# Expert weights of a mixture-of-experts kernel: rows regrouped to 4 KB pieces, and at most two pieces of 1 MB in flight

## What is computed

```python
h = rmsnorm(x, ln2_g[l]) * (1.0 + scale2) + shift2
probs = softmax(xt @ router_w);  sel = probs + router_b        # 64 experts, pick 1 group of 8, top 2 inside
def expert_block(args):
    xb, e = args
    return (jax.nn.silu(xb @ w1[e]) * (xb @ w3[e])) @ w2[e]    # w1, w3: 1024x512, w2: 512x1024
y = y.at[t_s].add(yp[dest] * w_s[:, None]);  x = x + gate2 * y;  return rmsnorm(x, final_g)
```

## Time and profile before

| | us |
|---|---|
| median of 3 runs (lowest, highest) | 1820.02 (1812.35, 1824.44) |
| the profiled execution, its own time | 1824.44 |
| its span, first to last instruction | 1822.6 |
| TensorE busy | 1229.9 (67%) |
| VectorE busy | 456.4 (25%) |
| chain that ended last: the stores `ys_dram<-arena` | 55% of the span |

### The profile page before, as it was taken

How to read it: one execution, slowest core, us unless ns; L and a number is a source line. 1 busy time by engine, 2 the same in 40 slices (tenths; PEclk the granted TensorE clock), 3 DMA queues, 4 the chain that set the end, 5 groups by cost and what they waited for, 6 DMA issues and landing times.

```text
span 1822.6 us, 31309 instructions
## 1 busy us (share of the span) xinstructions
PE 1229.9 (67%) x12648; PEld 649.3 (36%) x12649; DVE 456.4 (25%) x880; ACT 213.1 (12%) x537; POOL 182.9 (10%) x319
## 2 busy tenths in 40 slices
PE   4999999999455545767646585656645656754680
PEld 3544546455322322333323343323322323322340
DVE  1399763235511101111101120101110101100126
ACT  2300132111110000001000010000000000000014
POOL 2011200000010100101000011101001101100013
PEclk8999999999587776978877798777777878876795
DMA  9364704521988797777898649897889896699627
GB/s 353 143 208 139 280 0 162 182 93 61 366 340 338 305 422 306 304 295 266 346 421 329 265 181 418 327 415 294 341 343 416 322 421 255 235 420 413 261 95 279
DMA packets 104984, 517.72 MB, mean 284 GB/s; under 512 B 8745, under 2 KB 25657, under 8 KB 87416
## 3 DMA queue, kind: packets, MB, share of 16 engines
q1 hardware_dynamic: 78976, 471.04, 64.2%
q0 software_dynamic: 11984, 32.33, 5.0%
q10 hardware_dynamic: 13992, 13.90, 2.3%
HBM read 482.22 MB, written 35.01 MB: 284 GB/s over the span
## 4 chain that ended last, share of the span: by engine, by line
DMA 58%; PE 34%; DVE 5%; ACT 1%; issue 1%; ACTq 0%; SPq 0%; POOL 0%; POOLq 0%; DVEq 0%
DMA ys_dram<-arena 55%; PE banks L547 9%; PE banks L625 6%; PE banks L692 6%; PE banks L681 4%; PE banks L575 2%; DVE arena L1221 2%; PE banks L593 2%; DMA arena<-xh_dram,where 1%; PE banks L495 1%; DMA arena<-in_w_ada 1%; DMA arena<-in_x 1%; PE banks L641 1%; PE banks L698 1%; DVE arena L1251 0%
## 5 line engine op out<-in xcount | busy, mean ns | idle before, releaser
L692 PE MATMUL banks<-arena 128*32 128x256 f32 x3392 | 301.4, 516 | 450.2 <-DVE arena L1221 450.2
L681 PE MATMUL banks<-arena 128*32 128x256 f32 x6784 | 409.3, 395 | 27.4 <-issue 25.4
L692 PEld LDWEIGHTS banks<-arena 128*32 128x32 f32 x3392 | 138.3, 142 | 559.1 <-issue 528.3
L681 PEld LDWEIGHTS banks<-arena 128*32 128x32 f32 x6784 | 215.8, 114 | 189.6 <-issue 63.6
L1221 DVE TENSOR_TENSOR arena<-banks,arena 128x256 f32<-128x256 f32 x106 | 45.1, 426 | 841.3 <-DMA ys_dram<-arena 796.3
L547 PE MATMUL banks<-arena 128*128 128x512 f32 x352 | 157.4, 605 | 3.6 <-ACT arena L781 3.6
L443 POOL COPY where<-quarters 128x1 int32 (+1 forms) x108 | 19.9, 184 | 1222.7 <-ACT arena L855 1053.6
L841 ACT ACTIVATE arena<-banks 128x128 f32<-128x128 f32 x106 | 29.6, 279 | 849.7 <-issue 705.0
L969 DVE SCALAR_TENSOR_TENSOR arena<-arena 128x1024 f32<-128x1024 f32 x90 | 115.6, 1285 | 3.2
L446 POOL DMA_INDIRECT arena<-xh_dram,where x108 | 104.8, 970 | 87.7 <-POOL where L443 81.7
L625 PE MATMUL banks<-arena 128*128 128x512 f32 x256 | 111.4, 593 | 1.5 <-DVE arena L1002 1.5
(11 more groups left out here) (201 smaller groups left out, 667.5 us busy)
## 6 DMA issues: line engine op xcount, KB each, us to landing
arena<-in_exp_w SPq DMA_DIRECT2D x180, 2048.0 KB, 14.9
arena<-in_w_ada SPq DMA_DIRECT2D x12, 2048.0 KB, 11.2
arena<-in_exp_w SPq DMA_DIRECT2D x24, 1024.0 KB, 13.9
ys_dram<-arena ACTq DMA_DIRECT2D x106, 128.0 KB
ys_dram<-arena POOLq DMA_DIRECT2D x16, 512.0 KB, 10.0
arena<-in_x SPq DMA_DIRECT2D x2, 2048.0 KB, 19.9
arena<-in_dft SPq DMA_DIRECT2D x1, 4096.0 KB, 12.4
arena<-in_w_out SPq DMA_DIRECT2D x1, 4096.0 KB, 14.4
```

The costliest lines, as they stand in the source:

```text
L681: last = pe.matmul(h_p[32 * q:32 * q + 32, 0:2 * P].rearrange("p (a b) -> p a b", a=2), xt_s[:, k % 2, k // 2, :], w13[:, :, k, q * P:(q + ...
L692: last = pe.matmul(y_p[32 * q:32 * q + 32, 0:QUART], ff_t[:, k * BLK:(k + 1) * BLK], w2[:, k, q * QUART:(q + 1) * QUART], start=(k == 0), ...
```

## The change

- The channel order becomes 256q+2p+j everywhere. `w_in`, `router_w`, the columns of `ln_g`, `b_ada` and the modulation, `w1` and `w3` are loaded in that order; `chunk` takes every second channel of a quarter, `quarter_chunk` goes, and L1142 writes without a permutation. `w_in` and the router are now four transfers for each one before. The products for the first four slices of `w_ada` read contiguous columns where they read every fourth.
- `matrix` goes. All weights, in the loop too, are loaded in pieces of 1 MB: six for an expert, each 128 partitions x 2 runs of 4 KB. Each piece has a semaphore of its own.
- Before SP issues a piece in the loop it waits until the piece two before it (`AHEAD = 2`) has landed. The waits for the slot (`s_h13`, `s_yp`) stay.

```diff
+AHEAD = 2
         def d_cols(vector):
-            return vector.rearrange("(p k) -> p k", k=CH)
+            return vector.rearrange("(q p j) -> p q j", q=4, j=2)
...
         def chunk(view, k):
-            return view[:, k:D:CH]
-
-        def quarter_chunk(view, k):
             first = QUART * (k // 2) + k % 2
             return view[:, first:first - k % 2 + QUART:2]
...
-        s_w = [[sem(f"slot{i}_{what}_in") for what in ("w1", "w3", "w2")] for i in range(SLOTS)]
+        s_w = [[sem(f"slot{i}_{what}_in") for what in ("w1a", "w1b", "w3a", "w3b", "w2a", "w2b")] for i in range(SLOTS)]
...
-                sp.dma_start(w_in_s[:, :, f0:f1], w_in.rearrange("(p k) f -> p k f", k=CH)[:, :, f0:f1]).then_inc(s_win[part], 16)
+                for q in range(4):
+                    sp.dma_start(w_in_s[:, 2 * q:2 * q + 2, f0:f1],
+                                 w_in[q * QUART:(q + 1) * QUART, f0:f1].rearrange("(p j) f -> p j f", j=2)
+                                 ).then_inc(s_win[part], 16)
...
-                    src = (exp_w1, exp_w3)[u][bass.ds(e, 1), :, :].rearrange("e (p h c) f -> (e p) h (c f)", p=P, h=2)[:, h, :]
+                    src = (exp_w1, exp_w3)[u][bass.ds(e, 1), h * 512:(h + 1) * 512, :].rearrange("e (q p j) f -> (e p) q (j f)", q=2, j=2)
...
-                    sp.wait_ge(s_h13, end)
-                    for u in range(2):
-                        matrix(r * SLOTS + (SLOTS + slot), slot, u)
-                    sp.wait_ge(s_yp, end)
-                    matrix(r * SLOTS + (SLOTS + slot), slot, 2)
+                    for k in range(6):
+                        if k == 0:
+                            sp.wait_ge(s_h13, end)
+                        if k == 4:
+                            sp.wait_ge(s_yp, end)
+
+                        before, rounds = (slot, r + 2) if k >= AHEAD else ((slot - 1) % SLOTS, r + (2 if slot else 1))
+                        sp.wait_ge(s_w[before][(k - AHEAD) % 6], rounds * 16)
+                        piece(r * SLOTS + (SLOTS + slot), slot, k)
...
             for n, vec in ((LN1, ln1_g), (LN2, ln2_g)):
-                pool.dma_start(col[:, n, :], d_cols(vec)).then_inc(s_cols, 16)
+                pool.dma_start(d_tile(col[:, n, :]), d_cols(vec)).then_inc(s_cols, 16)
...
-            pool.dma_start(router_s, router_w.rearrange("(p k) e -> p k e", k=CH)).then_inc(s_rb, 16)
+            for q in range(4):
+                pool.dma_start(router_s[:, 2 * q:2 * q + 2, :], router_w[q * QUART:(q + 1) * QUART, :].rearrange("(p j) e -> p j e", j=2)
+                               ).then_inc(s_rb, 16)
...
-                        columns = ada_s[:, n % 2, k, q:HALF:4] if n < 4 else ada_s[:, n % 2, k, q * P:(q + 1) * P]
-                        last = pe.matmul(ps[32 * q:32 * q + 32, 0:P], c_wide[:, k, :], columns,
+                        last = pe.matmul(ps[32 * q:32 * q + 32, 0:P], c_wide[:, k, :], ada_s[:, n % 2, k, q * P:(q + 1) * P],
...
-                    for u in range(2):
-                        pe.wait_ge(s_w[slot][u], (r + 2) * 16)
+                    for k in range(4):
+                        pe.wait_ge(s_w[slot][k], (r + 1) * 16)
...
-                    v.tensor_scalar(xr[:, i % 4, :].rearrange("t (q p j) -> t q p j", q=4, j=2),
-                                    x2[:, i % 4, :].rearrange("t (p q j) -> t q p j", q=4, j=2),
-                                    rstd[:, 1, i:i + 1], None, ALU.mult).then_inc(s_xhat, 1)
+                    v.tensor_scalar(xr[:, i % 4, :], x2[:, i % 4, :], rstd[:, 1, i:i + 1], None, ALU.mult).then_inc(s_xhat, 1)
```

More of the change, by code:

```diff
@@ L182, in d_cols, with d_tile @@
         def d_cols(vector):
-            return vector.rearrange("(p k) -> p k", k=CH)
+            return vector.rearrange("(q p j) -> p q j", q=4, j=2)
+        def d_tile(view):
+            return view.rearrange("p (q j) -> p q j", q=4)
         def chunk(view, k):
-            return view[:, k:D:CH]
-        def quarter_chunk(view, k):
             first = QUART * (k // 2) + k % 2
@@ L315, in piece @@
                 if u < 2:
-                    src = (exp_w1, exp_w3)[u][bass.ds(e, 1), :, :].rearrange("e (p h c) f -> (e p) h (c f)", p=P, h=2)[:, h, :]
+                    src = (exp_w1, exp_w3)[u][bass.ds(e, 1), h * 512:(h + 1) * 512, :].rearrange("e (q p j) f -> (e p) q (j f)", q=2, j=2)
                 else:
                     src = exp_w2[bass.ds(e, 1), h * 256:(h + 1) * 256, :].rearrange("e (k p) d -> (e p) k d", k=2)
[L319 to L326, removed]
+                sp.dma_start(at(slot * EXPERT_FLOATS + k * 2048, 2, D), src).then_inc(s_w[slot][k], 16)
             for k in range(2):
@@ L406, in _ @@
             for n, vec in ((LN1, ln1_g), (LN2, ln2_g)):
-                pool.dma_start(col[:, n, :], d_cols(vec)).then_inc(s_cols, 16)
+                pool.dma_start(d_tile(col[:, n, :]), d_cols(vec)).then_inc(s_cols, 16)
             for n, m in ((BSH1, 0), (BSC1, 1), (BSH2, 3), (BSC2, 4)):
-                pool.dma_start(col[:, n, :], d_cols(b_ada[m * D:(m + 1) * D])).then_inc(s_cols, 16)
+                pool.dma_start(d_tile(col[:, n, :]), d_cols(b_ada[m * D:(m + 1) * D])).then_inc(s_cols, 16)
             for h in range(6):
                 pool.dma_start(bs_b[64 * (h % 2):64 * (h % 2) + 64, h // 2, :], sgu_b[h, :].partition_broadcast(64)).then_inc(s_small, 16)
-            pool.dma_start(router_s, router_w.rearrange("(p k) e -> p k e", k=CH)).then_inc(s_rb, 16)
+            for q in range(4):
+                pool.dma_start(router_s[:, 2 * q:2 * q + 2, :], router_w[q * QUART:(q + 1) * QUART, :].rearrange("(p j) e -> p j e", j=2)
+                               ).then_inc(s_rb, 16)
             pool.dma_start(router_bb, router_b.partition_broadcast(P)).then_inc(s_rb, 16)
@@ L424, in _ @@
             for k, m in ((SH2, 3), (SC2, 4)):
-                pool.dma_start(col[:, k, :], d_cols(mod_dram.ap()[m * D:(m + 1) * D])).then_inc(s_modcols, 16)
+                pool.dma_start(d_tile(col[:, k, :]), d_cols(mod_dram.ap()[m * D:(m + 1) * D])).then_inc(s_modcols, 16)
             pool.wait_ge(s_ss, TILES)
@@ L477, in ada_columns @@
                 pe.wait_ge(freed_d, freed_at[index[("ada", n)]][1])
-                half = 64 * (n % 2)
-                for lane in range(4):
+                for q in range(2):
                     for j in range(2):
-                        k = 4 * j + lane
-                        last = pe.matmul(ps[half:half + 64, k:k + 1], head_rows[:, n, j:P:2], ident[:, 32 * lane:32 * lane + 1],
-                                         start=True, stop=True, skip_group_check=True)
+                        for e in range(2):
+                            k, lane = 2 * q + j, 32 * (2 * q + e)
+                            last = pe.matmul(ps[64 * e:64 * e + 64, k:k + 1], head_rows[:, n, j:P:2], ident[:, lane:lane + 1],
+                                             start=True, stop=True, skip_group_check=True)
                 last.then_inc(filled, 1)
@@ L561, in _ @@
                     if g == index[("g", 0, 0)]:
-                        pe.wait_ge(s_win[0], 16)
+                        pe.wait_ge(s_win[0], 64)
                     if key[1] == 0:
@@ L568, in _ @@
                 elif kind == "b":
-                    pe.wait_ge(s_win[1], 16)
+                    pe.wait_ge(s_win[1], 64)
                     z_cols(ps, 2 * CONV + key[1] * P, key[2])
                 elif kind == "v":
-                    pe.wait_ge(s_win[2], 16)
+                    pe.wait_ge(s_win[2], 64)
                     i = key[1]
@@ L577, in _ @@
                 elif kind == "u":
-                    pe.wait_ge(s_win[3], 16)
+                    pe.wait_ge(s_win[3], 64)
                     z_cols(ps, 1024 + key[1] * P, key[2])
@@ L630, in _ @@
                     for j in range(4):
-                        last = pe.transpose(ps[:, j * P:(j + 1) * P], quarter_chunk(xr[:, i % 4, :], 4 * h + j), ident)
+                        last = pe.transpose(ps[:, j * P:(j + 1) * P], chunk(xr[:, i % 4, :], 4 * h + j), ident)
                     last.then_inc(filled, 1)
@@ L635, in _ @@
                     if i == 0:
-                        pe.wait_ge(s_rb, 32)
+                        pe.wait_ge(s_rb, 80)
                     for h in range(2):
@@ L720, in _ @@
                     hidden_transposes(lo)
-                    pe.wait_ge(s_w[slot][2], (r + 2) * 16)
+                    for k in range(4, 6):
+                        pe.wait_ge(s_w[slot][k], (r + 1) * 16)
                     pe.sem_inc(s_begun, 1)
@@ L919, in _ @@
                     ps = begin("column", n - 1)
-                    part = slice(64 * ((n - 1) % 2), 64 * ((n - 1) % 2) + 64)
-                    v.tensor_copy(col[part, (SH1, SC1)[(n - 1) // 2], :], ps[part, 0:CH]).then_inc(freed_d, 1)
+                    v.tensor_copy(col[:, (SH1, SC1)[(n - 1) // 2], 4 * ((n - 1) % 2):4 * ((n - 1) % 2) + 4], ps[:, 0:4]).then_inc(freed_d, 1)
                 if n == 2:
@@ L1068, in route @@
```

(2 more changed lines are left out.)

## The result

The changed kernel is no faster: 1839.12 us (median of 14 runs, 1820.31 to 1854.78) against 1819.67 for the kernel before (14 runs, 1812.35 to 1826.36). The ratio is 1.0079 with a 95% interval of 1.0049 to 1.0107, so it is slower by about 0.8%, inside the 1% that I had called no change. The ratio leaves out three slow executions of after (1850.93 to 1854.78 us) of the 17 on record, and the median of the other 14 is 1834.47 us, 15 us over before. I had forecast 1710, range 1640 to 1790, and given no change 0.05. The profiled execution of after has a span of 1837.1 us.

The account below looks back on a forecast made before the run. Stores slowed by weight traffic were taken to bound the expert loop. 1065/11.5 gives 93 loaded blocks, plus 13 fast ones of 80 us: loop 1145 against 1257, gain 112, so 1824.4 becomes 1712, median 1710, range 1640 to 1790.

Parts of the forecast that it names:

- The bound of before: Expert loop: of 106 blocks, 68 are paced by a store's landing and 38 by TensorE; loop 1257 us.
- B: Time the DMA needs for the expert loop: 1024 us before, forecast 1065 after (bounds 1024 and 1090).
- the identity: Expert loop: time = B + (106 - B/p) x 6.15, with p the mean pace of blocks run while the DMA works.
- The pace p of a loaded block: Expert loop: mean pace of blocks that run while the DMA works, forecast 11.5 us after 15.0 before.
- The row at 1724.38: Trace of before, late in the loop: a store beside the 4 MB x2 reload in 4 KB runs took 11.91 us.
- The price of the rows in B: Expert loop: 4 KB runs for w1 and w3 cost 4% of the DMA rate, raising B from 1024 to 1065.
- The price of the window: Weight loads in the loop: a piece needs 4.9 us against 5.2 us drain of two, so nothing is added.
- Rival 2: Weight loads: the window loses part of the rate, 3.2 to 3.4 us a piece, 1745 to 1798 us; chance 0.18.
- rival 3: Weight loads: the window starves the DMA, deciding from 3.45 us a piece; 2010 us at 3.95; chance 0.09.
- Rival 4: Loop stores: not shortened, pace 15, loop 1280 us, within 1% or just above; chance 0.06.
- The edits at nothing: Dense part: strides, POOL's column loads, router and w_in in four issues were hidden or free, adding nothing.
- The signs that I had named: Success: stores 8 to 12 us, DMA share about 0.92; failure: share under 0.9, TensorE waiting at under 400 GB/s.

Follow-up runs that it names:

- before_store_16: The kernel before with only its store changed, each block's result written as four stores: 1585.10 us, ratio 0.8708.
- no_window_store_16: The changed kernel without the wait for the piece two before, and with each block's result written as four stores: 1586.20 us, ratio 0.8712.
- no_window: The changed kernel without the two lines that make SP wait for the piece two before: 1708.71 us, ratio 0.9411.
- window_1: The changed kernel with AHEAD = 1, each piece issued when the one before has landed: 2456.72 us in its one run.
- window_4: The changed kernel with AHEAD = 4 in place of 2: 1709.15 us, ratio 0.9405.
- tiny_store: The changed kernel with only 8 rows of 1 KB stored of each block and the scratch buffer zeroed beforehand: 1596.4 us, ratio 0.8801.

## Why the prediction was wrong

**The bound of before** was read rightly: stores paced the loop, 68 loaded blocks at 15 us and 38 at 6.15 us. What I did not ask is why a store of 128 KB should be slowed that much. The sentence from the Trainium skill ("DMA: Bandwidth & Descriptors", section "Why a DMA increments its semaphore by 16 and not by 1") on how a transfer is spread over engines gave it, four of 16, and the four semaphore writes of each store agree. I used it only for the price of the DMA's work. before_store_16 shows that it was the cause of the bound. It was in B as well: of my two values I kept 1024 us, because it fitted the loop, and dropped 969; with the store spread and no window the loads are issued within 974 us (no_window_store_16). The agreement of the identity with the measurement was weak evidence, since the pace of 15.0 in it had come from the same 1257 us.

**The pace p of a loaded block** held in size, but not for the reason that I gave first. I took 11.5 us, from 11.91 in the earlier trace rows; no_window has 11.8 between the two stores above, with no limit on the queue at all. So the halved queue, which I had named, did nothing for it there; the rows of 4 KB did. The row at 1724.38, on which I leaned, had such rows beside it. In the changed kernel, too, no wait for a store exceeds 9.2 us; the stores became short.

**The price of the rows in B** came out near: B 1065 and p 11.5 gave a loop of 1145 us. In no_window the loop runs from 519 to 1658.4, 1139 us, and the time is 1709 where I forecast 1710. That it is so close is partly luck. There 98 blocks wait for a store and 8 do not, so by the identity B is 1090 and the mean p 11.1, and my two errors cancel. And it is the kernel without its window: the forecast was right for a kernel that was not the one changed.

**The price of the window** is the step that failed: "4.9 against 5.2: covered, with little to spare. Nothing is added". The 4.9 us was measured right (window_1). What was wrong is that I compared a piece that has the engines for itself with an average drain. A piece waits for the last of 16 engines. Work that sits on four of them, 1 us of it in two intervals of three, is harmless when many loads are queued, because the other twelve go on. With a window of two it is charged to all sixteen. The term that I put at nothing is 0.5 us a piece over my 2.96: 3.46, so B is not 1065 but 360 x 3.46 = 1246. window_4 and no_window show the same from the other side: without the limit the changed kernel takes 130 us less.

**The rivals.** Rival 2 said 3.2 to 3.4 us a piece and 1745 to 1798; rival 3 decided from 3.45. At the measured pace my own formula gives 1246 + 25 = 1271 us of loop against 1257, some 14 us slower; the loop of the profiled execution is 1274 us long (516.3 to 1790.1), and the kernel is 15 us slower. So the prices were right and the chances wrong: 0.09 for rival 3, with a margin of 0.3 us in 5.2, was too little. I had named the margin as small, and kept 0.50 for a case that needed every piece to stay inside it. Rival 4 (stores as slow as ever) did not happen.

**The edits at nothing** cost nothing that shows: the dense part ends no later (first weight load of the loop at 516.3 us, 519.05 before).

**The signs that I had named** came in part. SP waits for its own pieces and TensorE is late on weights, as for rival 2 or 3, but the DMA's share is 0.91, not under 0.9; it is what I had forecast for success. The sign in GB/s was the sharp one: pieces waited for at less than 400 GB/s, and it is 325.

## What to carry to other kernels

A limit on transfers in flight is paid at the slowest engine of each transfer. Before adding one, look for small transfers that sit on a few of the DMA engines, and compare the time of a transfer with such company, not alone, with the drain of the window. And where a small store takes five times its time under load, first ask over how many engines it is spread: here that one question was worth 13%, the reordering 6% before it and nothing after it, and the window of two cost time in every pair of runs. Read the DMA by its rate, not by its busy share.

## What the runs showed of the hardware

- A store whose outermost dimension is 4 loaded four of the 16 DMA engines only: four semaphore writes for each store in the records of its queue, and four of a load's writes 0.6 to 0.8 us late in window_1, some 3.5 us in the kernel before. The Trainium skill ("DMA: Bandwidth & Descriptors", section "Why a DMA increments its semaphore by 16 and not by 1") gives the rule that predicts it. Written as four stores of 32 rows, the same 128 KB left 64 writes and took the kernel from 1820 to 1585 us.
- ScalarE's store and SP's weights, on one engine, took turns packet by packet: a store packet of 1 KB (46 ns) every 650 ns beside rows of 16 KB (611 ns) and every 198 ns beside rows of 4 KB (159 ns), in the kernel before and in no_window.
- A piece of 1 MB alone takes 4.9 us from issue to landing (window_1), and with a second in flight and hardly a store beside them 5.3 in the median of 315 pieces (tiny_store).
- With the store spread, runs of 4 KB (1586.2 us) and of 16 KB (1585.1 us) give the same time.
